# Second mixer: raw chunks count half in the pacing of the filler products, two more of them in the opening, and the last oc product ahead of the convolution's low part

## Chip, cores and metric

The kernel runs on one core of a Trainium2 chip. The metric is the device time of one execution in microseconds (us). TensorE is PE in the profile (PEld is its weight load), VectorE is DVE, ScalarE is ACT, GpSimd is POOL, and SyncE (SP) only issues the loads.

## What is computed

The input is x, 256 tokens of 1024 numbers in float32. A first block of two layers (SwiGLU, a mixer of three attentions, SwiGLU) is followed by a second block of two layers, each with a second mixer:

```python
def hybrid_layer(x, norm_g, w_in, fox_b, ...):
    z = rms_norm_2(x, norm_g) @ w_in
    (fq, fk, fv, ff, f_gate, glu_in, c_gate,
     nq, nkc, nvc, nks, nvs, nkw, nvw, n_gl, n_gate) = jnp.split(z, split_points, axis=-1)
    o_a = fox_attention(heads(fq, 4), heads(fk, 4), heads(fv, 4), ff + fox_b) * jax.nn.silu(f_gate)
    o_b = conformer_conv(glu_in, conv_w, conv_b, conv_ln_g, conv_ln_b, conv_pw) * jax.nn.silu(c_gate)
    o_c = nsa_attention(heads(nq, 8), ...) * jax.nn.silu(n_gate)
    return x + jnp.concatenate([o_a, o_b, o_c], axis=-1) @ w_out
```

The fox attention has 4 heads with a decay that is a cumulative sum. The convolution has 31 taps over 256 channels, a layer norm, silu and a product with conv_pw. The nsa attention has 8 heads and adds three branches: one over compressed keys, whose weights are two matrices of 2048x256, and two that for 256 tokens are causal attention with different keys.

## The kernel before

All weights come as one stream of chunks of 128x1024 float32 (512 KB). SyncE loads a chunk into one of four raw buffers, the next one as soon as the chunk four places earlier has been read. A product is made of three passes with reduced operands: ACT writes the high part of a chunk (whi, line 283), DVE the low part (wlo, line 289), and `mm3` does the three matmuls (lines 337 to 339). Five whi and wlo buffers let ACT run up to five chunks ahead (`Stream.next` and `prepare`). An instruction of ACT or DVE stands in its queue where the program's Python made it, and an engine takes its queue in order.

One kind of chunk is not split: the eight of the compression weights (tag "cmp"). PE reads them straight from raw, in eight small matmuls a chunk (line 342, out of bl). They are called raw chunks here, R1 to R8. Behind them in the stream stand the chunks for the fox queries and keys and the gates; the first five are called S1 to S5. S1 uses the raw buffer that R5 had, and S5 the one that S1 had.

`mixer2` weaves three strands by hand. The main strand is `tiles()`, the filler products: R1 to R8, then S1 on. The second is 20 pairs of heads, each with scores, a row minimum (nmt, DVE, line 1585), two exponentials (ACT, line 362), transposes of wk (PE, line 347), their copy out of PSUM (ACT, line 350) and the product with the values (PE, line 342). The third is the side strands: the convolution's taps, the decay, the compressed branch and the outputs. An opening of four rounds transposes the queries and keys and takes one raw chunk a round. The loop over pairs i then calls `tick` three times a pair: it adds 22/54 to a debt, takes a step of the main strand for each whole unit of it, and takes one step of every side strand. When the main strand has ended, `late` gives the scores one bank (bank3) where they had two, because the four output banks are wanted, and ticks start the output blocks (tag "out", lhs k). The transposes have one bank (TT, bank5), which the copy of the pair before must have left.

The decay's strand passes the cumulative sum through cumh (ACT), cuml (DVE), three POOL instructions, fa (POOL) and four fb (ACT). `conv_out` does the product with conv_pw, writes tmp (cv, DVE), ysh (ACT) and ysl (DVE); output chunks k = 2 and 3 read ysh and ysl. `nsa_out(t)` multiplies oc by its gate (DVE, line 373), transposes it and writes qTh and qTl; `finale` is the one for t = 1.

Of the kernel before, what the change touches and what calls it, by code (L numbers as in the profile page):

```python
# [191 lines left out]
def pause(n):  # L192
    for _ in range(n):
        yield
# [12 lines left out]
def build(nc, W, gains, qkg, cst, tab1, tab2, x_in, out, widths, tags):  # L207
    ctx = ExitStack()
    with ctx:
# [47 lines left out]
        class Stream:  # L257
# [52 lines left out]
            def next(self, tag):  # L310
                c = self.at
                assert tags[c] == tag, (tags[c], tag, c)
                self.at += 1
                self.lows()
                while self.split < c + NSPLIT and self.split in self.landed and (
                        self.split < NSPLIT or self.split - NSPLIT in self.done_tok):
                    self.prepare()
                if c not in self.parts:
                    self.lows(0)
                if tag in WHOLE:  # L320
                    return c, raw[c % NRAW], None, self.parts[c]
                i = c % NSPLIT
                return c, whi[i], wlo[i], self.parts[c]
# [25 lines left out]
        def a_copy(dst, src, *tokens):  # L349
            return act.op(lambda e: e.activation(dst, src, ACT.Copy), *tokens)  # L350
# [13 lines left out]
        def tt(eng, dst, a, b, o, *tokens):  # L364
            return eng.op(lambda e: e.tensor_tensor(dst, a, b, o), *tokens)  # L365
# [10 lines left out]
        def parts_of(hi, lo, src, *tokens):  # L376

            h = a_copy(hi, src, *tokens)
            return h, tt(dve, lo, src, hi.bitcast(F), ALU.subtract, h, *tokens)
# [841 lines left out]
        def mixer2(norm, l, after, T):  # L1221
# [201 lines left out]
            def tiles():  # L1423
# [13 lines left out]
                for kv in range(2):  # L1437
                    for q in range(4):
                        c_, wr, _, ready = st.next("cmp")
                        for k in range(4):  # L1440
                            mm_ = q * 4 + k
                            for hf in range(2):
                                tok = mm(bank[32 * hf:32 * hf + 32, kv * 128:(kv + 1) * 128],
                                         bl32[:, kv, mm_ * 30:mm_ * 30 + 32],
                                         wr[:, k * 256 + hf * 128:k * 256 + (hf + 1) * 128], mm_ == 0, mm_ == 15,
                                         ready, toks["blk"][kv], edge, free, mark=(k == 3 and hf == 1))
                        st.done(c_, tok)
                        yield
                toks["hid"] = i, bank[0:64, 0:256].rearrange("p (a b) -> p a b", a=2), tok
                yield from col_pair("col2", H, norm.ready, take_fqk(0), M2)  # L1450
                yield from col_pair("col2", H, norm.ready, take_fqk(1), M2)
# [28 lines left out]
            def conv_out():  # L1480
# [20 lines left out]
                d = stt(tmp, bank[:, :].rearrange("p (a b) -> p a b", a=2), 0.5, rgc[:, :, :], ALU.mult, ALU.mult,  # L1501
                        toks["cgs"], tok, d)
                XB.give(i, d)
                _, low = parts_of(ysh[:, :, :], ysl[:, :, :], tmp, d)
                yield from pause(2)
                mixed[2:4] = [[low], [low]]
                yield

# [309 lines left out]
            main = tiles()  # L1818
            first = turn_n()
            decays = iter_chain(branch_gates(), decay())  # L1820
            for _ in range(4):
                next(decays)
                next(first)
                next(main)
                next(taps)
            drain(first)

# [7 lines left out]
            owed, main_left = [0.0], [True]  # L1835

            def tick():
                owed[0] += 22 / 54
                while owed[0] >= 1 and main_left[0]:
                    owed[0] -= 1  # L1840
                    main_left[0] = next(main, "end") != "end"
                for z in sides:
                    next(z, None)
                if not main_left[0] and owed[0] >= 1.2 and blocks and mixed[OUT2[4 - len(blocks)]]:
                    owed[0] = 0.0
                    blocks.pop()
                    next(ending)
# [233 lines left out]
```

How the kernel before makes its waits and increments, by code:

```python
    def wait(self, *tokens):  # L125
        for tok in tokens:
            if tok is None:
                continue
            if isinstance(tok, list):
                self.wait(*tok)
                continue
            sem, value = tok
            if self.seen.get(id(sem), 0) < value:
                self.seen[id(sem)] = value
                self.todo.append(lambda e, s=sem, v=value: e.wait_ge(s, v))
# [1 line left out]
    def op(self, emit, *tokens, mark=True):  # L137
        self.wait(*tokens)
        if not mark:
            self.todo.append(emit)
            return None
        self.count += 1
        self.todo.append(lambda e: emit(e).then_inc(self.sem, 1))
        return self.sem, self.count
# [99 lines left out]
        def load(dst, src, s, *tokens):  # L244
            sp.wait(*tokens)
            sp.todo.append(lambda e: e.dma_start(dst, src).then_inc(s, 16))
            dma_count[id(s)] = dma_count.get(id(s), 0) + 16
            return s, dma_count[id(s)]
```

## Time and profile before

| | |
|---|---|
| median of 3 runs | 1635.24 us (1633.99 to 1635.32) |
| profiled execution: time | 1636.7 us |
| profiled execution: span, first to last instruction | 1634.9 us |
| PE busy | 1594.5 us, 98% |
| DVE busy | 951.6 us, 58% |
| ACT busy | 801.9 us, 49% |
| POOL busy | 165.8 us, 10% |
| mean granted clock of PE | 0.994 |

A timeline row gives the start and the duration in us from the span's start, the engine, the line, the operation with what it writes and reads, and in brackets how long the engine had been idle before and what ended that. Layer 0's second mixer runs its pairs from about 1333 to 1430 us, layer 1's from about 1504 to 1608 us. Consecutive instructions of an engine overlap a little in these rows, so one instruction's share of a chain is the distance between starts.

### The profile page before, as it was taken

The numbers are of one execution on the slowest core, as the hardware profiler recorded it, in microseconds if no ns is written. First come the engines' busy times: TensorE is split into PE (matmuls) and PEld (weight loads), VectorE is DVE, ScalarE is ACT, GpSimd is POOL, SyncE is SP. The second block draws the span as 40 slices with busy tenths as digits, with TensorE's granted clock in tenths as the row PEclk, the third lists the DMA queues.
The fourth block names the chain that finished last, engine by engine and source line by source line (L and its number), as shares of the span: only waits on it lengthen the run. The fifth ranks groups of instructions, "written<-read, shape, count | busy, mean of one in ns | idle before, by whom it ended". The sixth has DMA issues, their size and how long they took to land. (4 is left out here: it accounts for less than half of the span.)

```text
span 1634.9 us, 23336 instructions
## 1 busy us (share of the span) xinstructions
PE 1594.5 (98%) x8942; PEld 1375.3 (84%) x8942; DVE 951.6 (58%) x1449; ACT 801.9 (49%) x1352; POOL 165.8 (10%) x187
## 2 busy tenths in 40 slices
PE   7999999999999999999999999999999999999897
PEld 6888899988888887888889988878888879878886
DVE  5555475444765545555456544665554688577865
ACT  6444464445364444444355454454443555453642
POOL 0000022211200000000021221120000301010100
PEclk9999999999999999999999999999999999999998
DMA  7666455343555555655546443446665453255421
GB/s 244 207 201 203 147 177 192 131 142 129 168 174 186 182 191 166 196 188 184 183 143 197 155 129 127 150 152 213 206 207 192 152 181 117 78 170 170 143 70 52
DMA packets 76431, 269.63 MB, mean 165 GB/s; under 512 B 8480, under 2 KB 9504, under 8 KB 76320
## 3 DMA queue, kind: packets, MB, share of 16 engines
q1 hardware_dynamic: 76320, 268.14, 49.9%
q8 instruction: 71, 1.16, 0.3%
q14 instruction: 40, 0.33, 0.1%
HBM read 267.06 MB, written 1.05 MB: 164 GB/s over the span
## 5 line engine op out<-in xcount | busy, mean ns | idle before, releaser
L289 DVE TENSOR_TENSOR wlo<-raw,whi 128x1024 fp32r<-128x1024 f32 (+4 forms) x468 | 564.9, 1214 | 414.4 <-ACT whi L283 371.2
L283 ACT ACTIVATE whi<-raw 128x1024 fp32r<-128x1024 f32 (+3 forms) x496 | 508.5, 1034 | 433.2 <-PE bank L339 408.3
L337 PE MATMUL bank<-whi,hh 128*128 128x512 f32 (+4 forms) x1312 | 497.8, 379 | 6.8 <-DVE hl L373 3.7
L339 PE MATMUL bank<-whi,hl 128*128 128x512 f32 (+4 forms) x1312 | 486.4, 371 | 0.0
L338 PE MATMUL bank<-wlo,hh 128*128 128x512 f32 (+4 forms) x1312 | 485.8, 370 | 0.0
L337 PEld LDWEIGHTS bank<-whi,hh 128*128 128x128 f32 x1312 | 248.1, 189 | 49.7 <-DVE hl L373 7.0
L339 PEld LDWEIGHTS bank<-whi,hl 128*128 128x128 f32 x1312 | 247.8, 189 | 40.3
L338 PEld LDWEIGHTS bank<-wlo,hh 128*128 128x128 f32 x1312 | 248.3, 189 | 37.3
L337 PE MATMUL bank<-hh,whi 128*128 128x256 f32 x480 | 142.1, 296 | 0.0
L339 PE MATMUL bank<-whi,gl 128*128 128x512 f32 x352 | 138.7, 394 | 0.0
L338 PE MATMUL bank<-wlo,gh 128*128 128x512 f32 x352 | 137.9, 392 | 0.0
L337 PE MATMUL bank<-whi,gh 128*128 128x512 f32 x352 | 137.4, 390 | 0.0
L338 PE MATMUL bank<-hl,whi 128*128 128x256 f32 x480 | 135.8, 283 | 0.0
L339 PE MATMUL bank<-hh,wlo 128*128 128x256 f32 x480 | 135.6, 283 | 0.0
L289 POOL TENSOR_TENSOR wlo<-raw,whi 128x1024 fp32r<-128x1024 f32 x28 | 67.2, 2400 | 269.7 <-ACT whi L283 240.0
L338 PEld LDWEIGHTS bank<-hl,whi 128*128 128x128 f32 x480 | 92.0, 192 | 0.5
L337 PEld LDWEIGHTS bank<-hh,whi 128*128 128x128 f32 x480 | 91.9, 191 | 0.5
L339 PEld LDWEIGHTS bank<-hh,wlo 128*128 128x128 f32 x480 | 91.8, 191 | 0.0
L347 PE MATMUL bank<-kc,wk 128*128 128x128 f32 x452 | 72.4, 277 | 10.4 <-ACT wk L350 6.3
L338 PEld LDWEIGHTS bank<-wlo,gh 128*128 128x128 f32 x352 | 66.1, 188 | 15.0
L337 PEld LDWEIGHTS bank<-whi,gh 128*128 128x128 f32 x352 | 66.1, 188 | 14.3
L339 PEld LDWEIGHTS bank<-whi,gl 128*128 128x128 f32 x352 | 66.2, 188 | 13.2
(295 smaller groups left out, 1672.3 us busy)
## 6 DMA issues: line engine op xcount, KB each, us to landing
raw<-W SPq DMA_DIRECT2D x464, 512.0 KB, 3.3
raw<-W SPq DMA_DIRECT2D x26, 384.0 KB, 3.5
raw<-W SPq DMA_DIRECT2D x8, 416.0 KB, 3.0
tab<-tab SPq DMA_DIRECT2D x6, 384.0 KB, 3.9
raw<-W SPq DMA_DIRECT2D x4, 426.0 KB, 3.1
raw<-W SPq DMA_DIRECT2D x6, 192.0 KB, 2.8
x<-x_in SPq DMA_DIRECT2D x2, 512.0 KB, 5.8
tab<-gains SPq DMA_DIRECT2D x2, 512.0 KB, 4.3
```

The source lines that it names most:

```text
L283: high = act.op(lambda e: e.activation(whi[i][:, 0:w], r[:, 0:w], ACT.Copy), self.landed[c], free)
L289: tok = (low or dve).op(lambda e: e.tensor_tensor(wlo[i][:, 0:w], r[:, 0:w], whi[i][:, 0:w].bitcast(F), ALU.subtract), self.landed[c], hig ...
L337: pe.op(lambda e: e.matmul(dst, ah, bh, start=start, stop=False), *tokens, mark=False)
L338: pe.op(lambda e: e.matmul(dst, ah, bl, start=False, stop=False), mark=False)
L339: return pe.op(lambda e: e.matmul(dst, al, bh, start=False, stop=stop), mark=mark)
L347: return pe.op(lambda e: e.transpose(dst, src, idn), *tokens, mark=mark)
```

## The change

Three edits, all in the second mixer. A raw chunk now yields 0.5, and `tick` adds 20/54, takes steps as long as its debt is above zero and may go below it; so a raw chunk costs half a step, and a step is taken when the debt becomes positive and not when it reaches one. The opening takes two raw chunks in its third and fourth round, six in all. In `conv_out` the high and the low part are written a step apart.

```diff
@@ -1445,7 +1445,7 @@
                                          wr[:, k * 256 + hf * 128:k * 256 + (hf + 1) * 128], mm_ == 0, mm_ == 15,
                                          ready, toks["blk"][kv], edge, free, mark=(k == 3 and hf == 1))
                         st.done(c_, tok)
-                        yield
+                        yield 0.5
                 toks["hid"] = i, bank[0:64, 0:256].rearrange("p (a b) -> p a b", a=2), tok
                 yield from col_pair("col2", H, norm.ready, take_fqk(0), M2)
                 yield from col_pair("col2", H, norm.ready, take_fqk(1), M2)
@@ -1501,8 +1501,10 @@
                 d = stt(tmp, bank[:, :].rearrange("p (a b) -> p a b", a=2), 0.5, rgc[:, :, :], ALU.mult, ALU.mult,
                         toks["cgs"], tok, d)
                 XB.give(i, d)
-                _, low = parts_of(ysh[:, :, :], ysl[:, :, :], tmp, d)
-                yield from pause(2)
+                high = a_copy(ysh[:, :, :], tmp, d)
+                yield
+                low = tt(dve, ysl[:, :, :], tmp, ysh[:, :, :].bitcast(F), ALU.subtract, high, d)
+                yield
                 mixed[2:4] = [[low], [low]]
                 yield
 
@@ -1818,10 +1820,12 @@
             main = tiles()
             first = turn_n()
             decays = iter_chain(branch_gates(), decay())
-            for _ in range(4):
+            for z in range(4):
                 next(decays)
                 next(first)
                 next(main)
+                if z > 1:
+                    next(main)
                 next(taps)
             drain(first)
 
@@ -1835,10 +1839,11 @@
             owed, main_left = [0.0], [True]
 
             def tick():
-                owed[0] += 22 / 54
-                while owed[0] >= 1 and main_left[0]:
-                    owed[0] -= 1
-                    main_left[0] = next(main, "end") != "end"
+                owed[0] += 20 / 54
+                while owed[0] > 0 and main_left[0]:
+                    step = next(main, "end")
+                    main_left[0] = step != "end"
+                    owed[0] -= 0.5 if step == 0.5 else 1
                 for z in sides:
                     next(z, None)
                 if not main_left[0] and owed[0] >= 1.2 and blocks and mixed[OUT2[4 - len(blocks)]]:
```

The first place is ACT's queue where the opening of layer 0 ends (layer 1 has the same rows with other buffers): whi0 to whi4 are the high parts of S1 to S5, wk,sm with bank3 are the exponentials of pair 0, with bank4 those of pair 1.

```order
+L283 ACTIVATE whi0_0<-raw1_0 128x1024 [waits s_raw1]
 L362 ACT_TABLE_LOAD [waits s_pe]
 L362 ACTIVATE wk_0,sm_0<-bank3,nmt_0 128x128 [waits s_dve]
 L362 ACTIVATE wk_0,sm_0<-bank3,nmt_0 128x128
+L283 ACTIVATE whi1_0<-raw2_0 128x1024 [waits s_raw2]
+L283 ACTIVATE whi2_0<-raw3_0 128x1024 [waits s_raw3]
+L283 ACTIVATE whi3_0<-raw0_0 128x1024 [waits s_pe,s_raw0]
+L283 ACTIVATE whi4_0<-raw1_0 128x1024 [waits s_pe,s_raw1]
 L350 ACTIVATE cumh_0<-bank6 128x256 [waits s_pe]
 L362 ACTIVATE wk_0,sm_0<-bank4,nmt_0 128x128 [waits s_pe,s_dve]
 L362 ACTIVATE wk_0,sm_0<-bank4,nmt_0 128x128
-L283 ACTIVATE whi0_0<-raw1_0 128x1024 [waits s_raw1]
```

S1's high part moved from behind pair 1's exponentials to ahead of pair 0's, and those of S2 to S5, which stood far below, now stand ahead of cumh and of pair 1's exponentials.

The second place is DVE's queue in layer 1 between the row minima of the last two pairs, where PE comes to the first output block. Before:

```order
L1585 TENSOR_REDUCE nmt_0<-bank3 128x2 [waits s_pe]
L1534 RECIPROCAL sm_0<-sm_0 128x4
L365 TENSOR_TENSOR oa_0<-bank7,sm_0 128x256 [waits s_pe,s_dve]
L373 SCALAR_TENSOR_TENSOR oa_0<-oa_0,stat_0,rgf_0 128x256
L373 SCALAR_TENSOR_TENSOR oa_0<-oa_0,stat_0,rgf_0 128x256 [waits s_dve]
L365 TENSOR_TENSOR cv_0<-cv_0,bank2 128x2x256 [waits s_pe]
L1585 TENSOR_REDUCE nmt_0<-bank3 128x2 [waits s_pe]
```

Of the change:

```order
L1587 TENSOR_REDUCE nmt_0<-bank3 128x2 [waits s_pe]
L373 SCALAR_TENSOR_TENSOR oc_0<-oc_0,stat_0,rgn_0 128x512
L1536 RECIPROCAL sm_0<-sm_0 128x4
L365 TENSOR_TENSOR oa_0<-bank7,sm_0 128x256 [waits s_pe,s_dve]
L373 SCALAR_TENSOR_TENSOR oa_0<-oa_0,stat_0,rgf_0 128x256
L373 SCALAR_TENSOR_TENSOR oa_0<-oa_0,stat_0,rgf_0 128x256 [waits s_dve]
L365 TENSOR_TENSOR cv_0<-cv_0,bank2 128x2x256 [waits s_pe]
L365 TENSOR_TENSOR qTl_0<-bank6,qTh_0 128x4x128 [waits s_pe,s_act]
L1587 TENSOR_REDUCE nmt_0<-bank3 128x2 [waits s_pe]
```

The gate product of oc for t = 0 and its transposed low part qTl now stand between the two row minima.

The third place is DVE's queue in layer 1 around the convolution's output, cv<-bank6. Before:

```order
L373 SCALAR_TENSOR_TENSOR cv_0<-bank6,rgc_0 128x2x256 [waits s_pe]
L365 TENSOR_TENSOR ysl_0<-cv_0,ysh_0 128x512 [waits s_dve,s_act]
L373 SCALAR_TENSOR_TENSOR oc_0<-oc_0,stat_0,rgn_0 128x512
L1515 RECIPROCAL sm_0<-sm_0 128x8
L365 TENSOR_TENSOR sm_0<-sm_0 128x8 [waits s_dve]
L365 TENSOR_TENSOR tab_0<-bank2,sm_0 128x512 [waits s_pe,s_dve]
L373 SCALAR_TENSOR_TENSOR oc_0<-oc_0,stat_0,rgn_0 128x512 [waits s_pool]
```

Of the change:

```order
L1517 RECIPROCAL sm_0<-sm_0 128x8
L365 TENSOR_TENSOR sm_0<-sm_0 128x8 [waits s_dve]
L365 TENSOR_TENSOR tab_0<-bank2,sm_0 128x512 [waits s_pe,s_dve]
L373 SCALAR_TENSOR_TENSOR cv_0<-bank6,rgc_0 128x2x256 [waits s_pe]
L373 SCALAR_TENSOR_TENSOR oc_0<-oc_0,stat_0,rgn_0 128x512 [waits s_pool]
L365 TENSOR_TENSOR ysl_0<-cv_0,ysh_0 128x512 [waits s_dve,s_act]
```

The oc product for t = 1, which waits for POOL, moved from four places behind ysl to just ahead of it; tab, which POOL reads, moved ahead of cv. On PE, the value product of the last pair now stands ahead of the conv_pw product, and the transposes of oc for t = 0 stand ahead of the last pair's scores, where before both stood between the conv_pw product and output chunk 2.

The pacing itself moves as follows. Before, pairs 0 to 3 each bring one raw chunk (R5 to R8) and pair 4 the first half of S1. Now pair 0 brings R7, R8 and the first half of S1. The last chunk of the main strand is taken in pair 17's third tick before, in pair 16's first now; the strand's end is seen in pair 18's third tick before, in pair 17's first now, so that the scores of pairs 18 and 19 have one bank, where only those of pair 19 had.

## Rows read from the trace of the kernel before

**Rows 1.** The page's costliest group: DVE's low parts, mean ns of one.

```profile
L289 DVE TENSOR_TENSOR wlo<-raw,whi 128x1024 fp32r<-128x1024 f32 (+4 forms) x468 | 564.9, 1214 | 414.4 <-ACT whi L283 371.2
```

**Rows 2.** Waits of PE, 1500 to 1636 us: total us, times, longest.

```profile
PE bank L347 <- ACT wk L350: 3.9, 4, 2.6
```

**Rows 3.** Timeline of PE, layer 1's second mixer, after the opening: start, us, engine.

```profile
1515.09 0.44 PE L347 MATMUL bank<-kc,wk 128*128 128x128 f32 x2 [2.62 <-ACT wk L350]
...
1516.29 0.28 PE L337 MATMUL bank<-hh,whi 128*128 128x256 f32 x1
...
1518.44 0.44 PE L347 MATMUL bank<-kc,wk 128*128 128x128 f32 x2 [0.57 <-ACT wk L350]
...
1519.08 0.36 PE L337 MATMUL bank<-hh,whi 128*128 128x256 f32 x1
...
1520.58 0.28 PE L342 MATMUL bank<-kTh,qTh 128*128 128x256 f32 x1
```

**Rows 4.** Timeline of ACT, the same stretch.

```profile
1505.26 1.28 ACT L362 ACT_TABLE_LOAD   x1
...
1507.58 0.37 ACT L362 ACTIVATE wk<-bank,nmt 128x128 f32<-128x128 f32 x1 [1.04 <-DVE nmt L1585]
...
1508.29 0.38 ACT L350 ACTIVATE cumh<-bank 128x256 fp32r<-128x256 f32 x1
...
1511.55 1.06 ACT L283 ACTIVATE whi<-raw 128x1024 fp32r<-128x1024 f32 x1 [0.86 <-DMA raw<-W]
...
1512.51 1.08 ACT L362 ACTIVATE fb<-cuml,kc 128x256 fp32r<-128x256 f32 x2
```

**Rows 5.** Loads into raw issued 1506 to 1516 us (x5); engines by stretch.

```profile
DMA to landing us min/median/max: 4.1/4.4/5.3
...
1509.00:1512.00 3.00, 2.81 (x37) 2.24 (x38) 3.00 (x9) 1.26 (x5) 2.44 (x4) 1.00 0.90 294
```

**Rows 6.** Timeline of DVE and of POOL, the same stretch.

```profile
1508.70 0.42 DVE L365 TENSOR_TENSOR cuml<-bank,cumh 128x256 f32<-128x256 f32 x1 [0.36 <-ACT cumh L350]
...
1509.43 0.42 DVE L1585 TENSOR_REDUCE nmt<-bank 128x2 f32<-128x256 f32 x1
...
1511.05 0.73 POOL L365 TENSOR_TENSOR cuml<-cuml,cumh 128x256 f32<-128x256 f32 x1
```

**Rows 7.** Timeline of PE, layer 0's second mixer.

```profile
1342.78 0.69 PE L347 MATMUL bank<-kc,wk 128*128 128x128 f32 x2 [1.93 <-ACT wk L350]
...
1349.02 0.28 PE L342 MATMUL bank<-kTh,qTh 128*128 128x256 f32 x1
```

**Rows 8.** Timeline of PE and of DVE, layer 1's last pairs.

```profile
1589.22 0.50 PE L342 MATMUL bank<-kTh,qTh 128*128 128x512 f32 x1 [0.81 <-ACT wk L362]
...
1594.35 0.50 PE L337 MATMUL bank<-whi,fqh 128*128 128x512 f32 x1 [0.56 <-DVE fql L365]
...
1587.43 0.68 DVE L1585 TENSOR_REDUCE nmt<-bank 128x2 f32<-128x512 f32 x1
...
1590.33 0.69 DVE L1585 TENSOR_REDUCE nmt<-bank 128x2 f32<-128x512 f32 x1 [0.29 <-PE bank L342]
```

**Rows 9.** Timeline of DVE, PE and POOL, layer 1, after the convolution's product.

```profile
1604.71 0.69 DVE L373 SCALAR_TENSOR_TENSOR cv<-bank,rgc 128x512 f32<-128x512 f32 x1 [3.31 <-PE bank L339]
...
1606.10 0.69 DVE L365 TENSOR_TENSOR ysl<-cv,ysh 128x512 fp32r<-128x512 f32 x1 [0.70 <-ACT ysh L350]
...
1606.71 0.75 DVE L373 SCALAR_TENSOR_TENSOR oc<-oc,stat,rgn 128x512 f32<-128x512 f32 x1
...
1607.51 0.66 PE L347 MATMUL bank<-kc,oc 128*128 128x128 f32 x4 [2.00 <-DVE oc L373]
...
1608.58 1.29 POOL L365 TENSOR_TENSOR oc<-oc,tab 128x512 f32<-128x512 f32 x1 [21.28 <-DVE tab L365]
```

**Rows 10.** Stretches of layer 0 and 1: us, busy by engine, PEclk, DMA share.

```profile
1342.70:1346.10 3.40, 3.32 (x16) 3.33 (x17) 2.25 (x6) 3.40 (x10) 0.00 (x0) 0.51 0.82 270
...
1515.00:1520.00 5.00, 4.34 (x36) 4.14 (x37) 3.47 (x5) 5.00 (x15) 0.00 (x0) 1.00 0.66 202
```

## Prediction

> **What bounds the kernel now.** I read the page first. PE is busy for 98% of the span, so the time changes by what the change does to PE's few waits, and all of its edits lie in the two second mixers. The costliest group of another engine, DVE's low parts, has 414 us of idle time ahead of it, so DVE has room on the whole [rows 1]. The list of PE's waits for the last 136 us says who causes them: the largest item is transposes that wait for ScalarE's copy of wk, 3.9 us in 4 waits, one of them 2.6 [rows 2]. Then the timeline of PE alone, around that long wait: PE stood still for 2.62 us until 1515.09 and for 0.57 us until 1518.44 [rows 3]. The same wait is in layer 0, 1.93 us until 1342.78 [rows 7]. At the end of the mixer there are waits of 0.81 and 0.56 us [rows 8] and one of 2.00 us [rows 9].
>
> Why does PE wait at 1515? The timeline of ScalarE tells it: ScalarE takes its queue in order, and its high part of S1 stood idle for 0.86 us on the load before it began at 1511.55 [rows 4]. The loads are why: five of them took 4.1 to 5.3 us, and the DMA engines were busy 0.90 of 1509 to 1512 at 294 GB/s [rows 5]. At that rate a chunk of 524 KB takes 524/294 = 1.78 us. PE is through with a raw chunk's eight small matmuls in less than that, so the loads are the limit of this stretch. Anything that takes them sooner meets the loads.
>
> **The opening, part by part.** R5 and R6 move into the opening, R7, R8 and S1 to pair 0. No work is added; the sum is over waits. The first place shown of the queues is what counts. ScalarE now has S1's high part ahead of pair 0's exponentials, and those of S2 to S5 ahead of cumh and of pair 1's. S5's load goes into S1's buffer: it can be issued only when S1's low part is written, and until it has landed everything behind it on ScalarE stands, above all cumh, the exponentials of pair 1, and the copy of pair 0's wk, for which PE's transposes of pair 1 wait. Step by step in layer 1:
>
> S1 lands when it did, at about 1511.5: its load is issued half a microsecond sooner, but the loads ahead of it fill the engines. High part 0.96 (1511.55 to 1512.51, start to start [rows 4]): 1512.5. The exponential's table load, 1.28 [rows 4], lay free in a gap before and now stands exposed behind it: 1513.8. Exponentials of pair 0, 0.71 (1507.58 to 1508.29): 1514.5. High parts of S2 to S4, 3 x 0.96: 1517.4. Meanwhile S1's low part, 1.2 [rows 1], ends at 1513.8, S5's load is issued then and takes 4.1 to 5.3 [rows 5]; I take 4.4, the median: 1518.2. High part of S5: 1519.2. Cumh 0.38: 1519.6, and cuml 0.42: 1520.05. The row minimum of pair 1 ended 0.73 after cuml before (1509.12 to 1509.85 [rows 6]): 1520.8, its exponentials 1521.5. The fb need POOL, whose third instruction ended 2.66 after cuml (1509.12 to 1511.78 [rows 6]): 1522.7. From the first fb to the transposes of pair 1 it was 2.58 (1512.51 [rows 4] to 1515.09 [rows 3]), and the same instructions stand there now: 1525.4.
>
> What has PE done by then? It has been through S1 and the first half of S2 and pair 3's scores. At 1520.58 the kernel before had done S1 and scores to pair 4 [rows 3]. It was ahead by transposes and values of pairs 0 and 1, scores of 4 and transposes of 2: 1.20 (1515.09 to 1516.29) and 0.64 (1518.44 to 1519.08). It was behind by half of S2, 1.50 (1519.08 to 1520.58). So the same work was done at 1520.58 - 1.84 + 1.50 = 1520.24, and the loss is 1525.4 - 1520.24 = **5.2 us**. The waits of 2.62 and 0.57 that the change could fill are inside that comparison.
>
> Layer 0: the transposes of pair 1 started at 1342.78. In layer 1 they come 10.3 later than before; here S1 was not waited for, so I take 10.0: 1352.8. The second half of S1 ended at 1349.02 [rows 7], the same work less 0.34 at 1348.7. Loss **4.1 us**.
>
> Then VectorE, which stood still behind S1's high part, is late by some 4 us with the row minima of pairs 2 to 5, and the copies of wk come after exponentials that wait for them. I estimate 1 us more of waits a layer, between nothing and 2: **2 us** for both.
>
> Bounds. Lowest: S1 lands 0.7 sooner, S5's load takes 4.1, nothing follows: 1.0 less a layer and the 2 us gone, so 7.3 for both. Highest: 5.3 for S5's load and 2 us of followers a layer, 15.1.
>
> The Trainium skill (DMA: Bandwidth & Descriptors, section Bandwidth) gives 341 GB/s for a transfer of 1 MB and about 358 GB/s as HBM's share of a core; here the rows show 294. By 350 GB/s a load would take 1.5 us, S5 would land by some 1517, ScalarE's own row of high parts would set 1517.4, and the loss would be 0.8 us a layer smaller. The Trainium skill (ScalarE: Activation LUTs, section What ACT_TABLE_LOAD costs) puts a table switch at 2.66 us with its drain, where the row has 1.28; by the page the chain of pair 0 would be 1.4 us later and the loss up to that much larger.
>
> **The last pairs.** Fillers run out a pair and a half sooner. The work that stood among the last pairs (the mean, the compressed branch, oc's transposes) fills pairs 17 and 18, and I expect no wait there: the 0.81 at 1589.22 [rows 8] goes. But the second place shown puts the oc product, 0.75 [rows 9], and qTl, 0.69 like ysl, between the row minima of the last two pairs. From the first (1587.43) VectorE was through with the queue between at 1590.33 - 0.29 = 1590.04 [rows 8], 2.6 later; now it takes 4.1. The last scores end some 2.9 after the first minimum in both (1590.33 less 1587.43, oc's transposes taking the place of the wait), so the last minimum is about 1.2 late, and the exponentials, the convolution's tanh, fqh and the first output block (1594.35) move with it. Gone from this place is also a compressed product, by my estimate 0.9 (two passes of a 512-wide matmul, 0.50 each in [rows 8]), which is work elsewhere and leaves a hole here. Net 1.2 + 0.9 - 0.81: **1.3 us** lost a layer, bounds 0 (VectorE's rows hidden behind PE's work) and 2.2.
>
> **The oc edit.** Before, after conv_pw's product PE did the last values, until 1605.51, and then stood 2.00 until oc for t = 0 was through: cv 1604.71, ysh, ysl 1606.10, oc 1606.71, transposes 1607.51 [rows 9]. Now the values stand ahead of the product, and output chunk 2 waits for ysl. Counted from the product's end T (about 1604.6): tab ends near T - 0.3, POOL's oc 1.29 to T + 1.1, the oc product 0.75 to T + 1.85, ysl to T + 2.55. So 2.55 of wait for 2.00: **0.55 us** a layer, of which 0.4 is the wait for POOL. If POOL were ready, ysl would be through at T + 2.2. No reader of the last oc gains: its transposes stand far below, under output blocks.
>
> **Sum.** 5.2 + 4.1 + 2 + 2 x 1.3 + 2 x 0.55 = 15.0. The profiled execution took 1636.7, of which 1634.9 were its span, so 1651.7; the median of the runs shown lies 1.5 under it: **1650.2, say 1650**.
>
> **Rivals.**
> A, the fillers fill. If S5 lands and S2 to S4 are split before PE needs pair 1's exponentials, the waits of 2.62 and 0.57, and 1.93 in layer 0, go and only 1.85 a layer at the end come back: 1635.2 - 5.1 + 3.7 = 1634, and with the end's waits at nothing 1630. It decides at S5's load: high part done by about 1513 instead of 1519. Against it, S1 itself was waited for until 1511.55 [rows 4]. Chance of faster 0.08, of within 3.3 us (0.2%, about what a measurement can tell) 0.05.
> B, slower but half. The loads run better when asked sooner, PE finds work in the queue's order, and the last pairs cost nothing: the lower bound of 7.3 alone, 1642, with 1638 to 1645 around it. Chance 0.22.
> C, my forecast, 1645 to 1656: 0.53.
> D, the clock. PE's granted clock was 0.51 for 3.4 us from 1342.7 on, right after the 1.93 us of waiting, and 1.00 in 1515 to 1520 after the 2.62 [rows 10]; these are the levels of 1.2 and 2.4 GHz. A stretch at half costs up to 1.7 us. Four longer waits a layer could bring two or three more such stretches: 1650 + 2 x 4 = 1658. Chance 0.12. The Trainium skill (TensorE: Matmul & The Clock Gate, Part 1) has the array's clock fall to 1.2 GHz when the engine has been idle; by it D is the rule, in the trace it held once of two.
>
> **How the numbers follow.** Slower 0.22 + 0.53 + 0.12 = 0.87, same 0.05, faster 0.08. The range reaches over most of B, C and most of D: 1640 to 1661, leaving out the 0.13 of A and no change, and some 0.07 at the far ends.
>
> **What would show it.** In the trace after: ScalarE idle on loads ahead of S1 and S5, cumh some 9 to 11 us later against pair 0's scores than now, PE's transposes of pair 1 after a wait of 2 us or more, with a wait ahead of pair 3's scores; VectorE idle some 3 us behind S1's high part; output chunk 2 starting on ysl after 2.4 to 2.7 us. I would be wrong if ScalarE's high part of S5 does not wait for its load or cumh comes soon after pair 0's exponentials; and the end's terms would be wrong if the first output block waits under 1 us.

## The result and the profile after

The changed kernel took 1653.72 us (median of 4 runs, 1649.35 to 1654.81), the kernel before 1634.87 on the same chip (1633.99 to 1635.32): ratio 1.0105, 95% interval 1.0091 to 1.0118, so some 17 us slower by the ratio (15 to 19 by its interval; the two medians are 18.9 apart), where 1650 with 1640 to 1661 around it stood in the prediction. The profiled execution is the shortest of the four, 1649.35 us with a span of 1647.6. PE is busy for 97% of it.

First the list of PE's waits from 1500 us on, which answers to [rows 2].

```profile
engine line waited for: us in total, times, longest us
PE bank L347 <- ACT wk L350: 5.2, 3, 2.9
PE bank L337 <- DVE wlo L289: 2.7, 1, 2.7
PE bank L337 <- DVE ysl L365: 2.3, 1, 2.3
PE bank L342 <- DMA raw<-W: 1.6, 4, 0.5
```

The wait for the copy of wk has grown (3.9 before), and two items are new: split chunk S1's low part, and the raw chunks themselves. PE's rows that waited in layer 1's opening say where; they answer to [rows 3].

```profile
start us, us, engine line op out<-in xcount [idle before <-releaser]
1513.35 1.07 PE L342 MATMUL bank<-raw,bl 128*32 128x128 f32 x16 [0.35 <-DMA raw<-W]
1514.96 1.07 PE L342 MATMUL bank<-raw,bl 128*32 128x128 f32 x16 [0.54 <-DMA raw<-W]
1517.01 1.07 PE L342 MATMUL bank<-raw,bl 128*32 128x128 f32 x16 [0.31 <-DMA raw<-W]
1518.44 1.07 PE L342 MATMUL bank<-raw,bl 128*32 128x128 f32 x16 [0.37 <-DMA raw<-W]
1522.20 0.51 PE L337 MATMUL bank<-hh,whi 128*128 128x256 f32 x1 [2.69 <-DVE wlo L289]
...
1524.85 1.43 PE L342 MATMUL bank<-tab,ls 128*128 128x256 f32 x4
...
1531.15 0.38 PE L342 MATMUL bank<-kTh,qTh 128*128 128x256 f32 x1 [0.85 <-ACT wk L362]
...
1534.81 0.44 PE L347 MATMUL bank<-kc,wk 128*128 128x128 f32 x2 [2.92 <-ACT wk L350]
```

The four raw rows are R5 to R8: PE waits for each of them, then 2.69 us for S1, and 2.92 ahead of pair 1's transposes. The waits of this opening add up to 8.0 us, against 3.9 before (0.19, 2.62, 0.57, 0.51); in layer 0 it is 8.1 (0.66, 0.64, 0.87, 2.98, 2.92) against 3.5 (0.66, 0.43, 0.25, 1.93, 0.26). The row at 1524.85 is the product that makes the cumulative sum, which cumh copies: it now stands behind the first half of S1. ScalarE's rows, beside [rows 4]:

```profile
1519.67 1.06 ACT L283 ACTIVATE whi<-raw 128x1024 fp32r<-128x1024 f32 x1 [5.78 <-DMA raw<-W]
1520.74 1.28 ACT L362 ACT_TABLE_LOAD   x1
1522.04 0.37 ACT L362 ACTIVATE wk<-bank,nmt 128x128 f32<-128x128 f32 x1
...
1522.74 2.94 ACT L283 ACTIVATE whi<-raw 128x1024 fp32r<-128x1024 f32 x3
1527.74 1.06 ACT L283 ACTIVATE whi<-raw 128x1024 fp32r<-128x1024 f32 x1 [2.06 <-DMA raw<-W]
1528.70 0.36 ACT L350 ACTIVATE cumh<-bank 128x256 fp32r<-128x256 f32 x1
1530.29 0.37 ACT L362 ACTIVATE wk<-bank,nmt 128x128 f32<-128x128 f32 x1 [1.22 <-DVE nmt L1587]
...
1532.21 1.09 ACT L362 ACTIVATE fb<-cuml,kc 128x256 fp32r<-128x256 f32 x2 [0.86 <-POOL cuml L365]
```

ScalarE stands for 5.78 us on S1's load and, after S2 to S4, 2.06 us on S5's, with cumh behind. At the end of the mixer, PE and DVE (beside [rows 9]):

```profile
1607.15 0.75 PE L347 MATMUL bank<-kc,wk 128*128 128x128 f32 x4 [2.00 <-ACT wk L350]
1608.37 0.80 PE L337 MATMUL bank<-whi,fqh 128*128 128x512 f32 x1 [0.46 <-DVE fql L365]
1622.16 0.47 PE L337 MATMUL bank<-whi,ysh 128*128 128x512 f32 x1 [2.27 <-DVE ysl L365]
```

```profile
1619.93 0.69 DVE L373 SCALAR_TENSOR_TENSOR cv<-bank,rgc 128x512 f32<-128x512 f32 x1 [0.70 <-PE bank L339]
1620.62 0.75 DVE L373 SCALAR_TENSOR_TENSOR oc<-oc,stat,rgn 128x512 f32<-128x512 f32 x1
1621.32 0.69 DVE L365 TENSOR_TENSOR ysl<-cv,ysh 128x512 fp32r<-128x512 f32 x1
```

2.46 us of waits at the last pairs (before: 0.81, 0.21 and 0.56, of which [rows 8] shows two) and 2.27 for ysl (before: 2.00 for oc). VectorE's cv, oc and ysl stand in a row and none waits for POOL.

### The profile page after: what moved, and what is told of

Its sections match the earlier page's. It is cut to its first block and busy times, and to the rows that moved or that the text cites. A ratio compares the mean times of both kernels' runs of the same rounds, so it can differ in the third digit from the quotient of the medians.

```text
span 1647.6 us, 23343 instructions
## 1 busy us (share of the span) xinstructions
PE 1595.6 (97%) x8942; PEld 1378.5 (84%) x8942; DVE 952.6 (58%) x1449; ACT 801.7 (49%) x1352; POOL 168.3 (10%) x187
## 5 line engine op out<-in xcount | busy, mean ns | idle before, releaser
L347 PEld LDWEIGHTS bank<-kc,wk 128*128 128x128 f32 x452 | 54.3, 141 | 27.6 <-ACT wk L350 11.5
```

Source lines behind the costliest of these rows:

```text
L347: return pe.op(lambda e: e.transpose(dst, src, idn), *tokens, mark=mark)
```

## One account for all kernels: idle time and the clock

The waits do not make up the whole difference, so each trace was put through the same two sums. One is PE's idle time, all gaps between its first and its last record; the 12.9 us of the span that lie outside these are nearly the same in all traces and are left out. The other is clock loss: over the span in steps of 0.85 us, PE's busy time times what PEclk (the granted clock as a share of full speed) lacks of 1.00. In us:

```
kernel         span    idle   clock loss
before        1634.9   27.3    6.7
after         1647.6   38.9   11.0
oc_only       1633.6   26.3    5.0
pace_only     1650.0   40.0   10.8
open_only     1644.5   35.2    9.4
cap_after     1656.2   43.8   14.1
ramp_after    1659.9   44.4   16.5
after_fb      1650.0   40.3   10.8
light_before  1635.5   27.5    6.8
light_after   1642.8   36.7    8.2
cap_before3   1638.5   28.8    9.9
heavy         1658.2   40.2   16.6
fb_late       1631.5   25.5    3.3
```

A line fitted through the 13 with the weight of idle held at one, span = 1601.9 + idle + 0.80 x clock loss, misses none by more than 3 us. With both weights left free the fit gives 0.72 and 1.21 and misses none by more than 2 us: idle time and clock loss rise together in these kernels, so the fit does not part them well. For the change itself the parts can be counted. Of the 12.7 us by which the span grew, 11.6 are idle time, and PE's busy time is 1.1 longer (1595.6 for 1594.5). The clock loss is 4.3 higher, for which the fitted line would give 3.4; that is 2.3 more than is there. Most of the cost in the two profiled executions is thus waits; the clock's part is 1 to 3 us by these two reckonings, and no run shows it more closely.

Six windows of the kernel after, each of them a stretch at a low clock, and one of the kernel before:

```profile
core 0: us, PE busy (x) PEld busy (x) DVE busy (x) ACT busy (x) POOL busy (x), PEclk, DMA share, GB/s
1341.30:1344.70 3.40, 3.40 (x15) 3.17 (x14) 1.98 (x2) 3.21 (x6) 0.00 (x0) 0.51 0.58 184
1351.50:1358.30 6.80, 5.57 (x26) 5.58 (x27) 4.38 (x8) 4.50 (x14) 1.79 (x1) 0.51 0.25 77
1426.30:1429.70 3.40, 2.84 (x9) 2.12 (x8) 2.58 (x4) 2.04 (x4) 0.00 (x0) 0.56 0.00 0
1521.50:1524.90 3.40, 2.70 (x13) 2.73 (x14) 1.96 (x3) 3.39 (x8) 0.00 (x0) 0.61 0.89 287
1535.10:1538.50 3.40, 3.40 (x22) 3.40 (x20) 1.96 (x4) 2.90 (x9) 0.27 (x1) 0.62 0.44 154
1607.30:1610.70 3.40, 2.94 (x10) 2.12 (x10) 2.39 (x4) 2.04 (x4) 0.00 (x0) 0.54 0.00 0
...
1568.00:1574.80 6.80, 6.80 (x23) 5.73 (x23) 3.50 (x9) 2.45 (x6) 0.00 (x0) 0.50 0.00 1
```

Each of the six begins near the end of a wait of about 2 us or more: those that ended at 1522.20, 1534.81 and 1607.15 in the rows above, and 2.98, 2.92 and 1.99 us in layer 0. Only the two waits for ysl (2.27) brought none. The levels are 1.2 and 2.4 GHz. The Trainium skill (TensorE: Matmul & The Clock Gate, Part 1) has the array's clock fall when the engine has been idle; here that held after six of eight such waits in the two mixers. In the kernel before it held after two of four (1.93 and the later 2.00), and the last row, its longest stretch at half speed, follows no wait at all: PE's last gap above 0.15 us, one of 0.24, lay 16 us back, and PE was busy in all of it. What brought that one stays open. The clock may also be why runs of one program differ: the other three runs of the kernel after have a mean clock of 0.989 or 0.990, the profiled one 0.992, and they took 4 to 5.5 us longer. They have no trace, and the relation is not general: oc_only's runs, below, took 1634.41 us at 0.994 and 1637.86 at 0.995.

## The experiments

Before each verdict: Q is the prediction's theory (ScalarE's queue with the high parts on loads ahead of the exponentials), L the loads' rate, T the mixer's end, K the clock. The recorded expectations call them theories. All ratios are to the kernel before on the same chip, where it took 1636.8, 1636.9 and 1636.6 us in the three groups.

**oc_only.** The hunk of the diff that touches conv_out, alone.

> The kernel before with the edit of the convolution's second part alone. Theories: Q, ScalarE's queue (its high parts of split chunks stand on loads ahead of pair 0's and pair 1's exponentials) costs most of the 18.8 us; T, the mixer's end (the last oc ahead of the low part, and fillers that run out sooner) costs most; L, the loads themselves are the limit, whatever ScalarE's order; K, half-speed clock stretches carry most. By Q this run costs what the wait ahead of output chunk 2 grows by, 0.3 (2.27 for 2.00 in the traces) to 0.55 a layer: 1635.5 to 1636.0. By T it is 1637.5 or more. By L and K as the kernel before, 1635 to 1636.

Measured: 1636.45 us, ratio 1.0000 (0.9991 to 1.0008). No loss. The wait of 2.00 for oc became two, shorter together:

```profile
1604.97 0.66 PE L347 MATMUL bank<-kc,oc 128*128 128x128 f32 x4 [0.61 <-DVE oc L373]
1606.60 0.62 PE L337 MATMUL bank<-whi,ysh 128*128 128x512 f32 x1 [0.98 <-DVE ysl L365]
```

So this edit costs nothing by itself. Of T only the fillers that run out sooner are left, and what they can carry is the growth of the waits at the last pairs and for ysl in the kernel after, 2.4 us of 11.6 for both layers.

**pace_only.** The pacing alone:

```
-                        yield
+                        yield 0.5
...
-                owed[0] += 22 / 54
-                while owed[0] >= 1 and main_left[0]:
-                    owed[0] -= 1
-                    main_left[0] = next(main, "end") != "end"
+                owed[0] += 20 / 54
+                while owed[0] > 0 and main_left[0]:
+                    step = next(main, "end")
+                    main_left[0] = step != "end"
+                    owed[0] -= 0.5 if step == 0.5 else 1
```

> The kernel before with the pacing alone (raw chunks count half, 20/54, paid in advance); the opening keeps its four raw chunks. ScalarE then has pair 0's exponentials ahead of S1, and S1 and S2 ahead of cumh, S3 behind pair 1's exponentials. By Q cumh comes at 1513 to 1514 instead of 1508.3 (two high parts behind one load), some 5 less late than in the kernel after, and its transposes of pair 1 lose about 2 a layer, the last pairs 1.3: 1640 to 1643. By T the last pairs alone: 1638 to 1640, with no new wait for wk. By L nearly all of the change, 1649 or more, since S5's load is asked for as early. By K it depends on how many half-speed stretches there are: 1.7 each.

Measured: 1652.92 us, ratio 1.0105 (1.0091 to 1.0118). All of the change's loss comes with this part, and of the forecasts only L's (1649 or more) has the number. Cumh is where Q had it, at 1513.4 on the clock of the kernel before (the layer begins 11.79 later, and the row below has 1525.15), but the cost is another: PE waits 4.48 us for S1 in layer 1, and 6.75 in layer 0.

```profile
1528.37 0.55 PE L337 MATMUL bank<-hh,whi 128*128 128x256 f32 x1 [4.48 <-DVE wlo L289]
```

```profile
1522.93 1.06 ACT L283 ACTIVATE whi<-raw 128x1024 fp32r<-128x1024 f32 x1 [2.76 <-DMA raw<-W]
1524.18 1.06 ACT L283 ACTIVATE whi<-raw 128x1024 fp32r<-128x1024 f32 x1 [0.20 <-DMA raw<-W]
1525.15 0.36 ACT L350 ACTIVATE cumh<-bank 128x256 fp32r<-128x256 f32 x1
```

```profile
1525.55 0.42 DVE L365 TENSOR_TENSOR cuml<-bank,cumh 128x256 f32<-128x256 f32 x1 [5.43 <-ACT cumh L350]
```

S1's high part is through at 1523.99, but its low part stands on VectorE behind cuml and pair 1's row minimum, which wait for cumh, and begins at 1527.01. Of the 4.48 us some 3 are this queue on VectorE, the rest is S1's load and splitting.

**open_only.** The opening alone:

```
-            for _ in range(4):
+            for z in range(4):
...
                 next(main)
+                if z > 1:
+                    next(main)
```

> The kernel before with the opening of six raw chunks alone; pacing 22/54 as before. ScalarE has S1's high part and the table load ahead of pair 0's exponentials, S2 ahead of cumh, S3 behind pair 1's exponentials. By Q pair 0's exponentials are at about 1514.5 (they were at 1507.6), cumh at 1516, pair 1's transposes at 1521 to 1522: 2 to 3 lost a layer, and 0.5 to 1.3 at the last pairs: 1640 to 1643. By T 1637 to 1639 (two fillers fewer at the end). By L the loads come as early as in the kernel after up to S2 and most is lost: 1646 or more.

Measured: 1646.28 us, ratio 1.0063 (1.0049 to 1.0077), some 10 us. Alone the two parts cost 17 and 10, together 17: as I read it they pay for the same thing, R5 to R8 taken early. PE has two new waits of over 2 us in each layer: for pair 0's exponentials (2.26 and 2.47), which stand behind S1's load as Q says, and for S1's low part (2.97 and 2.28), which Q left out. The number is L's (1646 or more), over Q's 1640 to 1643.

```profile
1521.36 0.58 PE L342 MATMUL bank<-kTh,qTh 128*128 128x256 f32 x1 [2.47 <-ACT wk L362]
```

**cap_after.** The kernel after, chunks taken up two deep until pair 2:

```
-                while self.split < c + NSPLIT and self.split in self.landed and (
+                while self.split < c + self.depth and self.split in self.landed and (
...
+            st.depth = 2
...
+                if i == 2:
+                    st.depth = NSPLIT
```

> The kernel after, but split chunks are taken up by ScalarE and VectorE at most two deep until pair 2: pair 0's exponentials stand ahead of S1's high part, cumh and pair 1's exponentials ahead of S3's. The order on TensorE and the loads asked for are those of the kernel after; only what stands in ScalarE's and VectorE's queues changes. By Q the wait for wk of pair 1 (2.92 in both layers) and 0.85 ahead of pair 3's scores shrink to under 1, the wait of 2.7 to 3.0 for S1's low part stays: 5 to 8 less than the kernel after, 1646 to 1649. By L TensorE waits for S2 to S4 instead and the time stays at 1652 to 1655. By T 1652 to 1655 as well. By K the time falls by 1.7 for each half-speed stretch that goes with the waits.

Measured: 1657.34 us, ratio 1.0129 (1.0115 to 1.0143), slower than the kernel after and above the range of each theory. The wait ahead of pair 1's transposes did shrink (1.70 and 1.22). But cumh, now free of the high parts, still has to wait for PE, where the product it copies stands behind S1, and came only 2.4 us sooner, counted from S1 on PE. And the high parts that were held back then stood in a row, with their low parts on VectorE ahead of pair 3's row minimum:

```profile
1537.11 0.44 PE L347 MATMUL bank<-kc,wk 128*128 128x128 f32 x2 [1.70 <-ACT wk L350]
...
1544.29 0.69 PE L347 MATMUL bank<-kc,wk 128*128 128x128 f32 x2 [4.40 <-ACT wk L350]
```

```profile
1530.97 0.38 ACT L350 ACTIVATE cumh<-bank 128x256 fp32r<-128x256 f32 x1 [4.38 <-PE bank L342]
```

```profile
1538.60 3.49 DVE L289 TENSOR_TENSOR wlo<-raw,whi 128x1024 fp32r<-128x1024 f32 x3 [2.41 <-ACT whi L283]
...
1542.41 0.41 DVE L1587 TENSOR_REDUCE nmt<-bank 128x2 f32<-128x256 f32 x1
```

**ramp_after.** The same with the depth raised by one at pairs 2, 4 and 6.

> The kernel after with split chunks taken up two deep, one more at pairs 2, 4 and 6 (two, three, four, five). Against two deep until pair 2 and five at once: four high parts and three low parts in a row stood there ahead of pair 3's row minimum and cost 4.4 us a layer. Theory Q (the burst costs, wherever it stands): spread out, the 4.4 goes and the 1.2 to 1.7 ahead of pair 1's transposes stays: 1646 to 1650, under the kernel after. Theory V (VectorE and ScalarE cannot make the parts and the softmax chain in the time that is left, however spread): S3 to S5 are late instead and the time stays at 1652 to 1658.

Measured: 1661.16 us, ratio 1.0145 (1.0131 to 1.0159). Q's 1646 to 1650 fails, and V's 1652 to 1658 is passed too: the 4.40 fell to 2.14, but new waits stand further on (0.70, 0.68, 2.06). They are waits for wk and kch; the late S3 to S5 that V named are not seen. The clock loss is among the largest of all, 16.5, so a part of the time may be the clock's.

**light_after and light_before.** Each raw chunk's load brings a quarter of its columns:

```
+                    w = 256 if tags[c] in WHOLE else widths[c]
-                    self.landed[c] = load(raw[i][:, 0:widths[c]], W[c, :, 0:widths[c]], s_raw[i],
+                    self.landed[c] = load(raw[i][:, 0:w], W[c, :, 0:w], s_raw[i],
```

> The kernel after, but each raw chunk's load brings 256 of its 1024 columns (the rest of the buffer is what the chunk before left there, so the compressed branch is computed from wrong weights); instructions, waits and their order are as in the kernel after. Theory L (the raw chunks are asked for faster than the DMA engines bring them, 1.78 us a chunk against 1.07 of TensorE's time, and S1 to S5 queue up behind them): the waits for raw loads go, S1 lands some 3 us sooner, its wait of 2.7 to 3.0 falls under 1, and the time falls by 8 to 12 us of the 17 to 19 that the change cost, to 1642 to 1646. Theory Q (ScalarE's order costs, whatever the loads): the burst of S2 to S5 with S5's load behind S1's low part stays as it is, and with it the wait of 2.9 for wk and that of 0.9 to 1: it falls by 2 to 5, to 1649 to 1652. Theory K: what falls beyond the waits is 1.7 for each half-speed stretch.

> The kernel before with the same short loads of raw chunks (the same part of the output wrong). It is the base for light_after. By L the 2.62 and 1.93 ahead of pair 1's transposes shrink (S1's load was late by 0.86 on ScalarE), 2 to 3 off: 1632 to 1634; and light_after less light_before is 5 to 9 us instead of 17 to 19. By Q that difference stays at 13 or more.

Measured: 1650.19 us, ratio 1.0086 (1.0072 to 1.0099), against 1635.37, ratio 0.9998 (0.9989 to 1.0007). The difference is still 14.8 us, where L had 5 to 9 and Q 13 or more, so what the raw chunks' loads take from those behind them is a small part, some 2 to 4 us of 17 to 19; the runs of light_after scatter from 1644.62 to 1652.81, and the profiled one is the fastest. The waits for raw chunks went, those for S1 and for wk did not:

```profile
1513.72 1.94 PE L343 MATMUL bank<-raw,bl 128*32 128x128 f32 x32
1518.11 0.36 PE L338 MATMUL bank<-hh,whi 128*128 128x256 f32 x1 [2.45 <-DVE wlo L290]
...
1526.77 0.38 PE L343 MATMUL bank<-kTh,qTh 128*128 128x256 f32 x1 [2.12 <-ACT wk L363]
...
1530.43 0.69 PE L348 MATMUL bank<-kc,wk 128*128 128x128 f32 x2 [2.92 <-ACT wk L351]
```

```profile
1515.58 1.06 ACT L284 ACTIVATE whi<-raw 128x1024 fp32r<-128x1024 f32 x1 [3.44 <-DMA raw<-W]
```

This shows what S1 waits for. Its load can start when R5's buffer is free, at 1512.15, and it is here at 1515.58, just as PE ends R8 (1515.66); high part, low part and hand-overs take 2.5 more. In the kernel after the same: R5 ended at 1514.42, S1's load took until 1519.67, PE ended R8 at 1519.51. Shorter raw loads only bring PE sooner to the same turn-round, load 3.4 to 5.2 and 2.5 of splitting, against 1.07 of PE's time for each of R6 to R8. What limits S1 is thus a load after all, not how fast the raw chunks come but how long its own takes once R5's buffer is free. Light_before has the waits of the kernel before in layer 1, but 1.94 where that profile has 2.62. The trace of oc_only, with full loads, has 1.94 there too, and in both ScalarE did not wait for S1's load: the late load was 0.7 of the 2.62, the other 1.9 was something else.

**heavy.** The opposite of the change, raw chunks counted one and a half (yield 1.5, 24/54, opening of four).

> The opposite of the change: the kernel before with raw chunks counted one and a half in the pacing, rate 24/54; the opening keeps four. R7 and R8 come later, behind pair 1's and pair 2's work, and S1 some two steps later. By L each load has more of TensorE's work beside it: the wait ahead of pair 1's transposes shrinks by 1 or so and nothing new appears: 1633 to 1635. By Q the same or a little better, since S1's high part stands behind the first fb: 1632.5 to 1635. By theory P (TensorE lacks work in the opening, and fillers there are what counts) it is slower, by the 1.07 of each raw chunk that is withheld there: 1638 to 1641.

Measured: 1658.77 us, ratio 1.0135 (1.0122 to 1.0149). P alone had the sign, but its 1638 to 1641 is at most a fifth of the 22 us, and most of the new waits are not where P put them. In layer 1 the opening's waits grew by some 2 us (1.18 ahead of pair 3's scores, 2.87 ahead of pair 1's transposes, 0.99 for a gate), those of the end by some 4: the fillers ran out 1.4 us ahead of the last scores, where before it was 4.4, and the mixer's end ran one after the other, with waits of 2.14, 1.27, 2.20 and 1.50. The clock loss is 9.9 higher as well.

```profile
1606.40 0.81 PE L347 MATMUL bank<-kc,oa 128*128 128x128 f32 x4 [2.14 <-DVE oa L373]
```

**cap_before3.** The kernel before, three deep until pair 4.

> The kernel before, with split chunks taken up at most three deep (five otherwise) until pair 4, so that S1's high part stands behind pair 2's exponentials and the copy of pair 0's and pair 1's wk, no longer between cumh's exponentials and fb. By Q the wait ahead of pair 1's transposes (2.62 and 1.93) falls by the 0.86 + 0.96 that S1's high part took there, and S1's own use is not late: 1632 to 1634, the first version under the kernel before. By the rival that the burst only moves (as two deep in the kernel after, where 4.4 us came back ahead of pair 2's transposes) the same or slower: 1635 to 1640.

Measured: 1640.05 us, ratio 1.0023 (1.0013 to 1.0032). Slower, at the upper end of the rival's range. The wait ahead of pair 1's transposes is 1.93 in both layers, where the kernel before has 2.62 and 1.93: only the 0.7 of the late load went, though S1's high part had left its place. And PE now waits for that high part:

```profile
1517.30 0.44 PE L347 MATMUL bank<-kc,wk 128*128 128x128 f32 x2 [1.93 <-ACT wk L350]
...
1520.40 0.55 PE L337 MATMUL bank<-hh,whi 128*128 128x256 f32 x1 [1.74 <-ACT whi L283]
```

**fb_late and after_fb.** What else stands ahead of that copy are decay's fb, which wait for POOL. Fa and fb are the last products of the decay's strand. The edit, in fb_late with oc_only's, in after_fb on the kernel after:

```
                 s2 = tt(pool, cuml[:, :], cuml[:, :], ch32, ALU.add, s1, s2)
-                yield
+                yield from pause(12)
                 got = []
```

> The kernel before with the edit of the convolution's second part, and decay's last part (POOL's two fa, ScalarE's four fb) twelve ticks later, so that they stand around pair 5 and no longer between pair 1's exponentials and the copies of wk. Theory F: the 1.93 ahead of pair 1's transposes is that copy standing behind three fb of 0.60 and the wait for POOL; without them the copy of pair 0's wk comes 1.7 to 2.0 sooner and the wait goes. Two layers: 3.5 to 4 less, and 0.4 a layer from the other edit: 1631.5 to 1634 where the kernel before has 1636.5. Rival: S1's high part and its load hold that copy, or the waits of pairs 5 and 6 grow by what the fb take there: 1635 to 1638.

> The kernel after with the same delay of fa and fb by twelve ticks; nothing else. Theory F: the wait of 2.92 ahead of pair 1's transposes shrinks by 1.7 to 2.0 plus what POOL's three instructions took (2.66 after cuml): it goes in both layers, 5 to 6 less: 1647 to 1649. Theory Q (the burst of S2 to S5 ahead of cumh): only 2 of it, the chain through pair 2's row minimum and exponentials ends little sooner, 1650 to 1652, and the wait of 2.7 to 3.0 for S1's low part stays in both theories.

Measured: fb_late 1635.72 us, ratio 0.9993 (0.9984 to 1.0002); after_fb 1650.92, ratio 1.0083 (1.0069 to 1.0097). In fb_late the time is the rival's (1635 to 1638), not F's. The wait shrank to 0.35 in layer 1 and 0.22 in layer 0, from 1.94 and 2.23 in oc_only, which shows its cause: fb with their wait for POOL. But 1.31 came back ahead of pair 2's transposes in layer 0, where ScalarE stands 1.07 on a load ahead of the copy:

```profile
1347.60 1.06 ACT L283 ACTIVATE whi<-raw 128x1024 fp32r<-128x1024 f32 x1 [1.07 <-DMA raw<-W]
1348.57 0.36 ACT L350 ACTIVATE wk<-bank 128x256 f32<-128x256 f32 x1
```

It has the least idle time and clock loss of all, and its interval still reaches to no change: a version that surely beats both kernels was not found. After_fb is some 3 us better than the kernel after, as Q had it (1650 to 1652) and not F (1647 to 1649): of the 2.92 ahead of pair 1's transposes 2.28 and 1.91 stayed. Its idle time is not less (40.3 against 38.9); the two intervals overlap, and its gain stays open.

## Why the prediction was right, point by point

The range was right, and so was the kind of the loss: PE waits longer in the opening because the raw chunks are taken sooner than the ring of buffers can follow. The steps were partly other than forecast, and the closeness of the sum is partly luck, as the last paragraph of this section shows.

**The opening in layer 1** came almost step by step. The stretch begins 8.66 us later than before (ScalarE's first row of it); less that, S1's high part began at 1511.01 (predicted 1511.55), pair 0's exponentials at 1513.38 (1513.8), S2 to S4 ended at 1517.02 (1517.4), cumh began at 1520.04 (1519.2) and pair 1's transposes at 1526.15 (1525.4). The 0.75 at the end is S5's load, 5.6 us instead of 4.4. Against the 1520.24 at which the prediction has the same work done before, the loss is 5.9 us, predicted 5.2; 8.0 - 3.9 = 4.1 of it are waits. In layer 0 pair 1's transposes began at 1352.73, predicted 1352.8, so the 4.1 was right to within half a microsecond by the prediction's own reckoning; the waits grew there by 8.1 - 3.5 = 4.6.

**What the order of steps hid.** The prediction put the loss down to one wait, pair 1's transposes behind S5's load on ScalarE. PE has three: the raw chunks (1.6 in layer 1), S1 (2.69) and the transposes (2.92), with 0.85 ahead of pair 3's scores. As I read it the end point was right because all lie on one chain from R5's buffer. The prediction also took cumh to be free once the high parts are through. PE's order says otherwise: the product that cumh copies stood ahead of S1 before (1506.07) and stands behind its first half now (1524.85 to 1526.28), so with no high part in the way cumh could have come at most 2.4 us sooner than it did (1528.70). That taking ScalarE's queue apart would give the time back was my reading of it, and cap_after and ramp_after refute it. The prediction's reason for the 2.62 ("high part of S1 stood idle for 0.86") was right for only 0.7 of it; light_before, oc_only and cap_before3 leave 1.93 or 1.94 without that load, and fb_late shows the rest to be fb and their wait for POOL.

**Followers** (2 us for both layers, bounds 0 and 4): the later waits on kch and wk are 0.3 each, four of them, where there was one of 0.34 and one of 0.24, so some 0.6 for both. **The last pairs**: 2.46 for 1.58 in layer 1 and 2.55 for 1.58 in layer 0, 0.9 and 1.0; predicted 1.3 each. The mechanism was right: the two last row minima are 3.80 us apart (1600.56 and 1604.36), where they were 2.90, and VectorE has no gap ahead of the second. The sign that was set for it was not: the first output block waits 0.46 us, under the 1 us that was to tell that these terms are wrong, because the 2.00 stands one step ahead, at the last transposes of wk. **The oc edit**: 0.27 a layer, predicted 0.55, and the wait for ysl is 2.27, under the 2.4 to 2.7 that were to show it. The step that failed is "of which 0.4 is the wait for POOL": POOL was through when VectorE came to oc. And the term's cause was wrong: oc_only has 1.59 us of waits there instead of 2.00, while pace_only, without that edit, has the 2.26 for ysl. The wait comes with the pacing, by which fillers run out sooner. Together the waits above 0.15 us grew by 4.1 + 4.6 + 0.6 + 1.9 + 0.5 = 11.7, which is the 11.6 of the table.

**The sum**: predicted 15.0, measured 12.7 in the profiled execution and 17 to 19 in the median. The time between the two has no trace; the longer runs have a lower mean clock, so rival D, which priced a stretch at 1.7, is the nearest candidate. D's count from the trace before, once of two waits, left out two waits of 2.00 and the 6.8 us at half speed that follow no wait. C and perhaps part of D are what happened. **A** fell: S1 was waited for, and S5's high part was through at 1528.70 - 8.66 = 1520.04 and not by 1513. **B** fell because the opening lost what was forecast and the mixer's end was not free.

**By layer** the sum was not as good. PE's rows of the profiled execution run 0.34 us ahead of those of the kernel before when layer 0's mixer begins, 8.65 behind when it is over and 12.67 behind at the end. Layer 0 thus cost 9.0 us, where the terms say 4.1 + 1 + 1.3 + 0.55 = 7.0, and layer 1 4.0, where they say 8.1. The waits grew alike, by 5.9 and 5.4. But PE's busy time is 3.1 longer in layer 0 and 1.4 shorter in layer 1. The clock goes with the first: its loss rose by 4.3 in layer 0 (1.7 to 6.0). In layer 1 it stayed at 5, because the kernel before has there the 6.8 us at half speed that no wait explains; for the 1.4 the rows show no cause. That the misses of +2 and -4 half cancel is luck, and with one trace of each kernel it stays open how much of them other executions share.

## What to carry to other kernels

A filler that takes 1 us of TensorE's time and a whole buffer of the load ring is no full filler: its price is the ring's turn-round, here a load of 3.4 to 5.2 us and 2.5 of splitting before the next split chunk behind it can be used. Before fillers are moved forward, count that chain from the buffer's release. When a copy is late, look first whether the product that it copies was moved behind the late chunk as well. A wait named after one copy can have several causes in the same queue; take them away one at a time, and look for where the time comes back. And add up a forecast by stage, and check it by stage: a good total can hide two misses of opposite sign.

## What was not expected of the hardware

How the clock behaves: its half-speed stretches come and go between traces of nearly the same program. At 1568 us the kernel before has 6.8 us of it, with no wait ahead, and light_before, which differs only in shorter loads of the raw chunks, half as much. In fb_late's 11 runs the time goes from 1632.7 us at a mean clock of 0.997 to 1638.69 at 0.994, though other programs, oc_only above all, do not show such an order. And the loads' rate is not fixed at the 294 GB/s that the sum used: in the kernel after

```profile
1518.10:1521.50 3.40, 1.07 (x16) 0.80 (x16) 0.67 (x1) 1.81 (x2) 0.00 (x0) 1.00 0.95 354
```

it was 354 GB/s. The Trainium skill (DMA: Bandwidth & Descriptors, section Bandwidth) has about 358 GB/s as a core's share when both cores of a memory domain stream. This kernel runs on one core and its stretch comes near that figure; whether it is a limit here, no run shows. The 8 loads issued in 1510 to 1525 took 5.0 us to landing in the median all the same, against 2.3 for light_after's raw loads of 128 KB. A load took 3.4 us where the one before it had nearly landed (issued at 1518.12 in the kernel before), and 5.7 us where three were still under way (1512.68 in the kernel after), so the rate alone does not say when the next buffer is here.
